# Gate rows turned on TensorE, one opening block, and attention outputs by rows in a two-network kernel

## What is computed

```python
for i in range(DEPTH):                       # DEPTH = 2
    mod_l = split(silu(c) @ w_mod[i] + b_mod[i], 6)       # six rows of 1024 for the latent tokens
    mod_c = split(silu(c_ctx) @ w_mod[i] + b_mod[i], 6)   # and six for the context tokens
    nl = modulate(rmsnorm(hl, norm1_g[i]), mod_l[0], mod_l[1])   # h * (1 + scale) + shift
    nc = modulate(rmsnorm(hc, norm1_g[i]), mod_c[0], mod_c[1])
    yc, yl = even_mixer(...) if i % 2 == 0 else odd_mixer(...)
    hl = hl + mod_l[2] * yl                  # gate row
    ...                                      # peer(): top-16 experts of 16384 for 8 heads
    hl = hl + mod_l[5] * peer(...)           # gate row
def mla_attend(q_n, q_r, k_n, k_r, v):       # in even_mixer, 8 heads, value width 64
    s = q_n k_n + q_r k_r
    p = softmax(s * MLA_SCALE)
    return p @ v
```

## Time and profile before

| | us |
|---|---|
| runs (3) | 4433.84, 4442.04, 4442.18; median 4442.04 |
| profiled execution | 4434.15 |
| its span | 4432.1 |
| PE busy | 4020.9 (91%) |
| DVE busy | 3193.4 (72%) |
| ACT busy | 2083.3 (47%) |
| POOL busy | 562.2 (13%) |

### The profile page before, as it was taken

One profiled execution on the slowest core, in us unless ns is written; L12 is line 12 of the kernel. 1 busy time (PEld: TensorE's weight loads), 2 busy tenths in 40 slices (PEclk: granted clock), 3 DMA queues, 4 the chain that ended last, 5 costly groups with the idle time before them and its releaser, 6 DMA issues. The chain is left out here.

```text
span 4432.1 us, 68779 instructions
## 1 busy us (share of the span) xinstructions
PE 4020.9 (91%) x24302; PEld 3580.4 (81%) x24302; DVE 3193.4 (72%) x7369; ACT 2083.3 (47%) x4104; POOL 562.2 (13%) x433
## 2 busy tenths in 40 slices
PE   6888899999899998889999999699887999988898
PEld 4568899999777776779998777598876989887687
DVE  6787899999677777668866667565586656558665
ACT  4334343676333334245575455444354444435453
POOL 0000024223222220004771000000000000000000
PEclk9998999999999998999999999899998999999899
DMA  6335588799999994757898888354434544443353
GB/s 225 99 115 189 141 295 287 275 318 332 346 332 336 315 321 143 247 176 208 227 244 254 256 252 267 141 185 152 132 104 164 187 163 186 158 128 122 130 194 132
DMA packets 426411, 939.83 MB, mean 212 GB/s; under 512 B 59706, under 2 KB 249338, under 8 KB 410506
## 3 DMA queue, kind: packets, MB, share of 16 engines
q1 hardware_dynamic: 370828, 801.86, 55.1%
q0 software_dynamic: 55296, 134.31, 9.6%
HBM read 842.60 MB, written 93.42 MB: 211 GB/s over the span
## 5 line engine op out<-in xcount | busy, mean ns | idle before, releaser
L161 PE MATMUL hidden<-hT_high__2,w_high__2 128*128 128x384 f32 (+1 forms) x1280 | 425.4, 332 | 29.5 <-DVE w_low__2 L173 15.1
L173 DVE TENSOR_TENSOR w_low__3<-w_raw__2,w_high__3 128x512 fp32r<-128x512 f32 x544 | 362.1, 688 | 122.3 <-ACT w_high__3 L168 105.0
L168 ACT ACTIVATE w_high__2<-w_raw 128x512 fp32r<-128x512 f32 x576 | 340.8, 625 | 223.6 <-DMA w_raw<-in_peer_u 82.4
L173 DVE TENSOR_TENSOR w_low__2<-w_raw,w_high__2 128x512 fp32r<-128x512 f32 x576 | 382.3, 688 | 75.2 <-ACT w_high__2 L168 74.0
L162 PE MATMUL hidden<-hT_low__2,w_high__2 128*128 128x384 f32 (+1 forms) x1280 | 420.7, 329 | 0.0
L163 PE MATMUL hidden<-hT_high__2,w_low__2 128*128 128x384 f32 (+1 forms) x1280 | 420.5, 328 | 0.0
L168 ACT ACTIVATE w_high__3<-w_raw__2 128x512 fp32r<-128x512 f32 x544 | 322.0, 624 | 86.3 <-PE side__2 L163 32.5
L161 PE MATMUL hidden__3<-hT_high__4,w_high__3 128*128 128x256 f32 x1152 | 327.0, 284 | 0.0
L163 PE MATMUL hidden__3<-hT_high__4,w_low__3 128*128 128x256 f32 x1152 | 323.3, 281 | 0.0
L162 PE MATMUL hidden__3<-hT_low__4,w_high__3 128*128 128x256 f32 x1152 | 323.3, 281 | 0.0
L161 PEld LDWEIGHTS hidden<-hT_high__2,w_high__2 128*128 128x128 f32 x1280 | 244.1, 191 | 32.2 <-ACT queries L1329 14.8
(11 more groups left out here) (995 smaller groups left out, 12142.1 us busy)
## 6 DMA issues: line engine op xcount, KB each, us to landing
w_raw<-in_peer_u SPq DMA_DIRECT2D x128, 512.0 KB
w_raw<-in_peer_v SPq DMA_DIRECT2D x128, 512.0 KB
w_raw__2<-in_peer_u SPq DMA_DIRECT2D x128, 512.0 KB
w_raw__2<-in_peer_v SPq DMA_DIRECT2D x128, 512.0 KB
activated_dram<-activated SPq DMA_DIRECT2D x128, 192.0 KB
routing_dram<-routing SPq DMA_DIRECT2D x24, 1024.0 KB
routing_chunk<-routing_dram SPq DMA_DIRECT2D x16, 1536.0 KB
activated_again<-activated_dram SPq DMA_DIRECT2D x128, 192.0 KB
```

The costliest lines, as they stand in the source:

```text
L161: nc.tensor.matmul(out, lhs[0], rhs[0], start=start, stop=False, skip_group_check=True)
L168: return nc.scalar.activation(high, src, ACT.Copy)
L173: return nc.vector.tensor_tensor(low, src, high.bitcast(F32), ALU.subtract)
```

## The change

It has three parts.

1. **Opening as one block.** `load` and `modulation` become `front`, whose SP queue issues the small `c_cols`, the weights as 16 pieces of 512 KB through a ring of 10 (in DRAM the weights now lie piece by piece), behind them the residual tiles and constants, and then the store of the SiLU rows. `Pieces`, the class of the mixers' weight queue, is moved up and used for it. The four bias additions, 16 transposes and the scales are the same.
2. **Gate rows turned by PE.** `sp_store` no longer writes single elements: PE turns the [128, 8] columns into [8, 128] rows (`pe_turn`), ACT copies them out of PSUM, and SP stores eight runs of 512 bytes for each row. In the first mixer this stands at steps `gates_at + 4` (PE, ACT) and `gates_at + 6` (SP), in the expert stage at 34 (PE), 35 (ACT) and 36 (SP), in the odd mixer at `gate_at + 1` and `gate_at + 3`, and for the last row at `NUM[-1] + 10` and at the queue's end.
3. **Attention by rows.** The turned exponentials are now the stationary operand (128 columns) and v moves (64 columns), so that the output has queries in partitions. The division by the sum moves from the probabilities to ACT's copy of the output. Once for eight heads PE turns the tile of 128 queries and 512 columns in four transposes, ACT makes its high and DVE its low part. The score banks are two and no longer three, and turned probabilities and turned tiles share two banks.

```diff
+            sp.dma_start(cc[:, :, :], w["c_cols"]).then_inc(c_loaded, 16)
+            for n in range(pieces.raws):
+                pieces.sp_load(sp, n)
...
+            for n in range(pieces.raws, len(sources)):
+                pieces.sp_load(sp, n)
+            for (to, frm), s in zip(loads, landed):
+                sp.dma_start(to, frm).then_inc(s, 16)
+            sp.wait_ge(silu_done, 2)
+            sp.dma_start(w["silu_rows"], plain_rows[:, :]).then_inc(rows_stored, 16)
...
-                if items and s == last_gates + 1:
-                    side_products.sp_store(sp, 2, [(0, 5, 0), (0, 5, 1)], rows_stored)
+                if items and s == gates_turn_at + 2:
+                    sp.wait_ge(rows_kept, 1)
+                    side_products.sp_store(sp, turned_rows, 5, (0, 1), rows_stored)
...
+                if items and s == gates_turn_at:
+                    pe.wait_ge(kept, sum(query_at[p] + QB < s for p in range(4)))
+                    side_products.pe_turn(pe, ident, 2, 5, (0, 1), side[:, 0, :], rows_turned)
...
+                if items and s == gates_turn_at + 1:
+                    act.wait_ge(rows_turned, 1)
+                    nc.scalar.activation(turned_rows, side[0:KC, 0, 0:2 * P], ACT.Copy).then_inc(rows_kept, 1)
...
+    def pe_turn(self, pe, ident, finished, g, vs, out, turned):
+
+        pe.wait_ge(self.own, finished)
+        for v in vs:
+            last = self.nc.tensor.transpose(out[0:KC, v * P:(v + 1) * P], self.m["columns"][:, g * KC:(g + 1) * KC, v],
+                                            ident[:, :])
+        last.then_inc(turned, 1)
+
+    def sp_store(self, sp, rows, g, vs, stored):
+
+        for v in vs:
+            sp.dma_start(self.m["rows"][v, g * D:(g + 1) * D].rearrange("(c p) -> c p", p=P), rows[0:KC, v * P:(v + 1) * P]) \
+                .then_inc(stored, 16)
...
-                        last = nc.tensor.matmul(out_part(o), v[:, c, h * MLA_V:(h + 1) * MLA_V],
-                                                pT[:, o % 2, c * P:(c + 1) * P], start=(c == 0), stop=(c == chunks - 1))
+                        last = nc.tensor.matmul(out_part(o), pT[:, o % 2, c * P:(c + 1) * P],
+                                                v[:, c, h * MLA_V:(h + 1) * MLA_V], start=(c == 0), stop=(c == chunks - 1))
                     last.then_inc(out_ready, 1)
+                for g in range(4):
+                    if i == H * g + H + 4:
+                        pe.wait_ge(out_kept, H * (g + 1))
+                        turned_free(pe, 1, g)
+                        for c in range(4):
+                            last = nc.tensor.transpose(turned_bank(1, g)[:, c * P:(c + 1) * P],
+                                                       attended[:, g % 2, c * P:(c + 1) * P], ident[:, :])
+                        last.then_inc(tile_turned, 1)
...
-                    high_part(nc, column(a_high, o), out_part(o)).then_inc(out_high, 1)
+                    act.wait_ge(inverted, o + 1)
+                    if g >= 2 and h == 0:
+                        act.wait_ge(tile_turned, g - 1)
+                    nc.scalar.activation(attended[:, g % 2, h * MLA_V:(h + 1) * MLA_V], out_part(o), ACT.Copy,
+                                         scale=inv_sum[:, o % 6:o % 6 + 1]).then_inc(out_kept, 1)
...
-                if 0 <= i - 1 < U:
-                    if k >= 3:
-                        dve.wait_ge(probs_turned, k - 2)
-                    nc.vector.tensor_scalar(probs[:, k % 3, 0:keys_of(k)], ex[:, k % 3, 0:keys_of(k)],
-                                            inv_sum[:, k % 3:k % 3 + 1], None, ALU.mult).then_inc(probs_ready, 1)
```

374 lines of the change are left out of this document (214 added, 160 removed).

## The result

The changed kernel takes 4424.19 us (median of 17 runs, 4412.60 to 4438.33), the kernel before 4447.26 in as many. The ratio is 0.9946, 95% interval 0.9935 to 0.9957: 24 us faster by the ratio, 23 between the medians. Two later comparisons gave 0.9931 (0.9905 to 0.9956) and 0.9942 (0.9920 to 0.9965). The sign of the forecast was right; the gain is about six tenths of the 41 us that were forecast, and 4424 lies outside the range of 4380 to 4418. (A few executions that took over 1.3 times as long were disturbed and count nowhere.)

What follows compares the result with a forecast made beforehand. PE, busy for 4020.9 of 4432.1 us, was taken to set the time. Terms of -12, -4.7, -6, -10 and -8 sum to -40.7, giving 4393.5 or 4401.3, middle 4397; range 4380 to 4418.

Steps and rivals of the forecast that it cites:

- odd mixer: Odd mixer's gate-row store: the wait behind it goes and numerators start 7.0 us earlier, plus 1 for the clock; -8 us.
- attention: Attention with turned operands: passes drop from 0.127 to 0.08 us, less the cost of added transposes; PE nets -6 us.
- base: Whole kernel's starting time: profiled execution of 4434.15 us and median of 4442.04, giving 4393.5 and 4401.3 after the terms.
- opening: Start of kernel: weights issued at about 1.2, next stage starts at about 36.8 instead of 48.98; -12 us.
- first mixer's stores: First mixer's gate stores: DVE's wait of 4.71 us for a side tile goes and counts in full; -4.7 us.
- expert stage: Expert stage: the 13.7 us stall behind the stores goes, while PE takes a new wait before slot 35; -10 us.
- rival B: Attention: loading 128 full rows sets the pass at 0.111 us, so it gains about 1, total 4402; chance 0.15.
- rival E: Attention: two score banks make PE wait, leaving it at the lower clock; about 60 us slower, 4457; chance 0.03.
- C: Three store places: behind each removed stall DVE is late next, so half of 22.7 us is lost, 4408; chance 0.15.
- D: Whole change gains more: opening -16, expert stage -13.2, attention -9.7, clock never falling -5 more, 4381; chance 0.12.
- F: Row stores stay slow and hold the queues as before, so 22.7 us are not won, 4420; chance 0.05.

Runs made afterwards that it cites:

- late turns: Expert stage's gate rows turned by PE in slot 38 instead of 34, in the whole change (ratio 0.9929) and in the change without attention by rows (0.9924).
- e8: Whole change with six loads of c, each waited for, put ahead of the opening as a delay: 4431.73 us, ratio 0.9960 to the kernel before.
- e7: Whole change with three banks for the attention scores instead of two: 4420.68 us, ratio 0.9937 to the kernel before.
- e3: Kernel before with the attention by rows alone: 4457.49 us, ratio 1.0014 to the kernel before.
- e9: Whole change with the expert stage's two gate rows turned in slot 38 instead of 34: 4419.87 us, ratio 0.9929 to the kernel before.
- e2: Kernel before with only the gate rows turned by PE: ratio 0.9951 to the kernel before, 22 us faster.
- e6: Whole change run again, unaltered: 4418.90 us, ratio 0.9931 to the kernel before.
- e1: Kernel before with the opening block of the change alone: 4435.89 us, ratio 0.9969 to the kernel before.
- e4: Kernel before run once more, unaltered: ratio 0.9997; its trace is 12.3 us longer than the first one of the same program.
- e15: Kernel before run a third time, unaltered: ratio 1.0004; its trace is 23.3 us longer than the first one of the same program.
- e13: Whole change run a third time, unaltered: ratio 0.9942 to the kernel before.

## Why the prediction was wrong

Two terms were too large, the odd mixer's (8, shown 2.6) and the attention's (6, shown 2.0), one cost was missing (3.7, in code that the change doesn't touch), and the base was 9 us too low. The sum again, with what the seventeen traces show in place of each term: mean of the traces with the part, less the mean of those without it. The late turns are left out of the expert stage's term and e8 out of the opening's; the attention's compares traces that all have the gate rows turned by PE, without e7 (alone, e3 against the other four, it is -2.4).

| term | forecast | shown |
|---|---|---|
| opening | -12 | -12.0 |
| first mixer's stores | -4.7 | -4.6 |
| attention by rows | -6 | -2.0 |
| expert stage | -10 | -11.2 |
| odd mixer | -8 | -2.6 |
| second network, 3395:3960 | 0 | +3.7 |
| sum | -40.7 | -28.7 |

The three comparisons of whole kernels give -24 (-19 to -29), -31 (-20 to -42) and -26 (-16 to -36), so the sum lies inside all three intervals, at the edge of the first; whether the 2 or 3 us between it and their mean are real stays open.

**Opening: right in size, by luck.** The next stage was put at 36.8 and stands at 36.52, but not for the reason given. The working let the loads end last: weights at 28.1, residual tiles at 35.2, and 1.6 us of scales, store and the block's end behind them. In the trace everything has landed by about 31 (the queue moved 413 GB/s from 10 to 20 us, more than the 370 taken as the bound), and PE's products, which the sum held to be over with the weights, end at 33.5. Behind them come 3.0 us of additions, transposes and scales. The last engine was ready 1.7 us earlier than the sum's last load, and the tail was 1.4 us longer than the sum's: that the two nearly cancel is chance.

**First mixer: right**, by the step that only DVE's 4.71 counts, since DVE is the late engine at 177.43.

**Expert stage: right in mechanism and nearly in size.** A PE wait of 5 to 7 us was forecast, and 7.11 is there; the stall is gone. The clock, which was to stay up, falls behind the new wait too (0.58 for 4 us). e9 shows that most of the new wait is DVE's lateness and that 2.5 us needn't be.

**Odd mixer: the failed step is "DVE copies it in 1.29, so the numerators can start at about 1817.8".** It took the idle time of one trace, 8.43, as the cost of the store, and let DVE copy v as soon as the projection ended. But DVE has decay products, a low part and a side product ahead of it in program order, so 3.80 us of waiting are left in the change (3.8 in e2 and e6 too). And the stall isn't 8.43 as a rule: in e1 and e3, which still have the old store, PE waited 6.8 and 6.6, in e4 6.2 and in e15 6.0. What the stretch gives is 2.6.

**Attention: the failed step is a cost put at nothing, the clock; and the gain that is there was priced by two misreadings that cancel.** The sum took 8 x (0.127 - 0.08) off a unit. Neither price is the distance of two passes. The 0.127 is 1.02 / 8, which has the two ends of the group in it; within it the old passes were 0.109 apart. The new ones are 0.112 apart, as in the earlier trace rows with 128 moving columns (0.111), and not 0.08. So the swap makes no pass faster, rival B's price was right, and the rows of two partitions were the wrong neighbours: that fewer columns move behind them doesn't make 128 full rows load faster. The Trainium skill, "TensorE: Matmul & The Clock Gate", section "LDWEIGHTS (loading the stationary operand)", had it: columns divided by 1.2, an estimate of 107 ns for 128 columns; the trace agrees with that rule, at 0.112. A unit still became 0.32 us shorter (2.51 to 2.19), near the 0.38 of the sum, but at the ends of the three groups and not in the passes; why they are shorter isn't shown. In the three traces in which the clock of this stretch is 0.92 (after, e6, e9) it is 6.9 to 7.1 us shorter than in the first trace of before, 5.2 against the mean of those with gate rows and the old attention (-1.8). That much of the -6 was right.

What takes it back was rival E's means, the clock, and not its cause: e7 shows that the banks aren't it. In four of the eight traces with the attention by rows the clock of the stretch is 0.83 to 0.88, in the old attention it was 0.91 to 0.93 in all that were looked at, and that takes 4 to 8.5 us back. E was priced at 60 us for the whole stretch at the lower level, with a chance of 0.03; it came in slices, in every second trace.

**The base.** The forecast was made from one profiled execution (4434.15) and a median of three (4442.04). Over 29, 25, 11 and 28 runs the kernel before has medians of 4448.7, 4452.2, 4448.8 and 4451.2. The forecast's middle stood on 4438, and the runs beside the changed kernel had 4447.3: of the 27 us between 4397 and 4424, 9 are this alone and 12 the terms above. The other 6 are not accounted for; they are the difference between -28.7 and the first comparison's -24, and about what its interval allows.

**The rivals.** C (half of what the stores give is lost again) is not what happened: e2 keeps 22 of the 23 us that its first reading gives. But its sign, a new wait of several microseconds on DVE where a stall was, stands in two of three places (7.11 and 3.80), and it is one of the two reasons why the odd mixer gives 2.6 and not 8. D needed everything and is out. F is out: the stores no longer hold the queues. What none of them named is the cost outside the changed stages: 3.7 us for moving the places at which PE's code is fetched. The range was too narrow because it was made of the terms' own bounds alone: the base, 9 us off, and costs outside the changed stages, 3.7, had no width in it, and the odd mixer's and the attention's terms had theirs from a single execution, while the same program's untouched stretches differ by up to 25 us between two of them.

## What to carry to other kernels

Before a stall in one trace is booked as a gain, look at what its engine has next in program order once the stall is gone, and ask for a second execution: an idle time of 8.43 was 6.0 to 6.8 in four others. When a stage ends where it was forecast, look at which engine ends it: here it was PE and not the loads. For a changed operand order, take the pass's price from a row with the same number of rows and columns in the stationary operand, however many columns move, and compare the distance of two passes with a distance, not with an average that has the ends of a group in it. When an edit of a few microseconds is measured, part of what comes out (here 3.7 us) can be the shift of instruction fetches in code that was not touched; a few idle instructions put in early show it.

## What the runs showed of the hardware

- A fetch of 16 KB of PE's instructions 3.6 to 4.2 us behind the first load of a block goes with data that ACT can start on after 6.2 to 6.4 us and not after 4.8 to 5.4, in 8 traces of 8 against 9 of 9. 18 small matmuls in the opening, 3600 us earlier, switch it on or off.
- The granted clock of the same stretch of the same program can be 0.92 in one execution and 0.83 in another (attention, e6 and e13), 8.5 us apart on 94.
- fp32 passes with 128 stationary columns of 128 rows start 0.11 us apart whether 64 columns move behind them (0.112 in the change) or 128 (0.111).
- Stores of single elements had held the DMA engines at 0.96 for 63 GB/s; eight runs of 512 bytes for each row leave 0.56 at 175 in the same place.
